# The causal mask of the prompt's attention: an addition by VectorE in PSUM in the place of a matrix product

## What is computed

```python
s = q @ k.T * HEAD_DIM ** -0.5          # 512 x 512 for each head
s = where(k_pos <= q_pos, s, -inf)      # the causal mask
p = exp(s - max(s)); p = p / sum(p)
o += gate[branch] * (p @ v)
```

## Time and profile before

| what | value |
|---|---|
| median of 3 runs | 2102.17 us (2101.37 to 2103.06) |
| the profiled execution's own time | 2100.33 us |
| its span in the profile | 2098.4 us |
| TensorE busy | 1946.2 us (93% of the span) |
| VectorE busy | 1146.9 us (55%) |
| ScalarE busy | 828.4 us (39%) |
| GpSimd busy | 692.4 us (33%) |
| mean granted TensorE clock | 0.966 of full speed |

### The profile page before, as it was taken

How to read it: one execution, slowest core, us unless ns; L and a number is a source line. 1 busy time by engine, 2 the same in 40 slices (tenths; PEclk the granted TensorE clock), 3 DMA queues, 4 the chain that set the end, 5 groups by cost and what they waited for, 6 DMA issues and landing times. The chain is left out here.

```text
span 2098.4 us, 38046 instructions
## 1 busy us (share of the span) xinstructions
PE 1946.2 (93%) x15341; PEld 1819.3 (87%) x15341; DVE 1146.9 (55%) x1931; ACT 828.4 (39%) x1809; POOL 692.4 (33%) x470
## 2 busy tenths in 40 slices
PE   6999798988889999999999996988987999999998
PEld 6999556987679999999999984678965999999998
DVE  3588755553344555555528876555533455555554
ACT  4594355443433232313146823544444341313130
POOL 2335434230033333333323552443200333343331
PEclk8999899999999999999999997999999999999999
DMA  4310520423322222222222132132342322222221
GB/s 152 102 62 21 163 67 16 112 81 113 109 72 84 87 81 81 81 81 81 81 83 82 62 96 84 50 78 62 102 131 64 95 81 81 81 81 81 87 86 55
DMA packets 200635, 175.75 MB, mean 84 GB/s; under 512 B 11356, under 2 KB 198030, under 8 KB 200334
## 3 DMA queue, kind: packets, MB, share of 16 engines
q1 hardware_dynamic: 200354, 173.30, 27.2%
q10 hardware_dynamic: 108, 0.03, 0.0%
HBM read 162.67 MB, written 10.62 MB: 83 GB/s over the span
## 5 line engine op out<-in xcount | busy, mean ns | idle before, releaser
L427 POOL TENSOR_TENSOR WX<-RAW,WX 128x2048 fp32r<-128x2048 f32 (+2 forms) x48 | 222.5, 4635 | 567.8 <-ACT WX L423 567.8
L2393 DVE TENSOR_TENSOR sq<-sq 128x288 f32<-128x288 f32 x128 | 157.0, 1231 | 196.8 <-ACT sq L2362 196.8
L427 POOL TENSOR_TENSOR m_wl<-RAW,m_wh 128x2048 fp32r<-128x2048 f32 x36 | 166.4, 4623 | 285.1 <-ACT m_wh L423 285.1
L439 PE MATMUL bank<-UH,m_wl 128*128 128x288 f32 x640 | 188.8, 295 | 0.0
L438 PE MATMUL bank<-UL,m_wh 128*128 128x288 f32 x640 | 188.8, 295 | 0.0
L437 PE MATMUL bank<-UH,m_wh 128*128 128x288 f32 x640 | 188.7, 295 | 0.0
L439 PE MATMUL bank<-UH,WX 128*128 128x288 f32 x576 | 170.1, 295 | 0.0
L438 PE MATMUL bank<-UL,WX 128*128 128x288 f32 x576 | 169.8, 295 | 0.0
L437 PE MATMUL bank<-UH,WX 128*128 128x288 f32 x576 | 169.7, 295 | 0.0
L423 ACT ACTIVATE WX<-RAW 128x2048 fp32r<-128x2048 f32 (+1 forms) x48 | 92.0, 1917 | 173.5 <-PE bank L439 150.8
L2415 DVE TENSOR_TENSOR XT<-XT,OT 128x288 f32<-128x288 f32 x128 | 156.3, 1221 | 4.4
(11 more groups left out here) (389 smaller groups left out, 5904.0 us busy)
## 6 DMA issues: line engine op xcount, KB each, us to landing
RAW<-in_w_up SPq DMA_DIRECT2D x32, 1024.0 KB, 5.3
RAW<-in_w_down SPq DMA_DIRECT2D x32, 1024.0 KB, 5.0
RAW<-in_w_in SPq DMA_DIRECT2D x20, 1024.0 KB, 5.2
R<-in_cache_nsa_kv SPq DMA_DIRECT2D x128, 64.0 KB
HT<-in_cache_nsa_kv SPq DMA_DIRECT2D x128, 64.0 KB, 2.7
RAW<-in_w_in SPq DMA_DIRECT2D x6, 1056.0 KB, 5.2
R<-in_cache_nsa_kv SPq DMA_DIRECT2D x48, 128.0 KB, 3.0
out<-R SPq DMA_DIRECT2D x10, 512.0 KB, 5.4
```

Of the source, the lines that this page charges most:

```text
L427: eng.tensor_tensor(S.granule(S.wl, i, w)[:, chunks], S.granule(S.raw, i, w)[:, chunks], S.granule(S.wh, i, w)[:, chunks].bitcast(F32), AL ...
L439: ins = pe.matmul(out, wl[:, c, cols], ah[:, c, n], start=False, stop=(c == KC - 1))
L2393: dve.tensor_tensor(relu[n % 4], relu[n % 4], relu[n % 4], ALU.mult).then_inc(sem("relu_squared"), 1)
```

## The change

The two bf16 products of a unit are taken out of `scores`, the second score product now ends its accumulation and increments `scored`, and VectorE adds the mask before it looks for the maximum: one `tensor_tensor` over the diagonal blocks of both heads, 128 partitions x 2 x 128 elements, PSUM in and out, the mask read from SBUF and repeated over the heads. It goes through `step`, so VectorE waits for its own addition before the `tensor_reduce`. In the constants, the bf16 identity and bf16 mask, each 64 columns of the fp32 array, give way to one fp32 mask of 128 columns, so the array keeps its size and the places of the others.

```diff
@@ _constants
-    put("ident16", _halved(np.eye(P)))
-    put("causal16", _halved(np.where(i[None] > i[:, None], NEG, 0.0)))
+    put("causal", np.where(i[None] > i[:, None], NEG, 0.0))
@@ scores(n), TensorE
                         for v in range(NKV):
                             k = slice(v * HD, (v + 1) * HD)
-                            pe.matmul(bank[2 * (n % 2) + v][:, 0:w], QT[k, g, t * P:w], KT[k, b, 0:w], start=True, stop=False)
-                        for v in range(NKV):
-                            ins = pe.matmul(bank[2 * (n % 2) + v][:, t * P:w], ident16, causal16,
-                                            start=False, stop=True)
+                            ins = pe.matmul(bank[2 * (n % 2) + v][:, 0:w], QT[k, g, t * P:w], KT[k, b, 0:w], start=True, stop=True)
                         ins.then_inc(sem("scored"), 1)
@@ VectorE
                             dve.wait_ge(sem("scored"), n + 1)
                             both = psum[:, n % 2 * 1024:n % 2 * 1024 + 1024].rearrange("p (v k) -> p v k", v=NKV)[:, :, 0:w]
+
+                            own = both[:, :, w - P:w]
+                            step(dve, dve.tensor_tensor(own, own, const("causal").unsqueeze(1).to_broadcast([P, NKV, P]), ALU.add),
+                                 "dve_done")
                             dve.tensor_reduce(nmax[:, 2 * n:2 * n + 2], both, AX, ALU.max, negate=True).then_inc(sem("maxed"), 1)
```

More of the change, by code:

```diff
@@ L23 @@
 F32R = mybir.dt.float32r
-BF16 = mybir.dt.bfloat16
 I32 = mybir.dt.int32
@@ L70 @@
 CONST_W = {}
-def _halved(a):
-    return (np.asarray(a, np.float32).view(np.uint32) >> 16).astype(np.uint16).view(np.float32)
 def _constants():
@@ L202, in build @@
         ident, ones, ones64 = const("ident"), const("ones"), const("ones64")
-        ident16, causal16 = const("ident16").bitcast(BF16), const("causal16").bitcast(BF16)
         G_ATTN, G_MLP, G_HG, G_KC, P_B1, P_LBA, P_OM, P_LNOM, P_HB = 0, 8, 16, 17, 18, 22, 26, 30, 34
```

## The result

The changed kernel takes 2115.98 us (median of 4 runs, 2113.22 to 2116.99) against 2102.61 us: 13.4 us slower. The ratio of the runs is 1.0062, its 95% interval 1.0045 to 1.0079. Forecast were 2114 us and 12.0 us.

The account below looks back on a forecast made before the run. Two loops through the engines, not TensorE's busy time, were taken to bound the kernel; addition delays less the earlier `scored` and slack gave 6.0 and 5.9 us in two layers, 12.0 on 2102.17: 2114 us, range 2108 to 2120.

Parts of the forecast that it names:

- loop B: Scores, maximum, exponentials, ScalarE's copy, turning products, later scores: once for two units, 6.75 us at 512 columns, 0.24 more after.
- loop A: VectorE and ScalarE, once a unit: maximum, exponentials, reciprocals, next maximum; 2.80 us at 512 columns, 0.46 more after.
- The faster rival: TensorE's list is the bound, the addition hides in VectorE's idle time: 7.7 us less, 2094.5; chance 0.07.
- The addition, 0.46 us: VectorE's mask addition and wait for itself delay each unit's maximum by 0.46 us, 0.42 of it the addition.
- The upper bound of 0.52: VectorE's addition at its dearest: a two-input form of 479 ns plus 0.04 for the wait.
- the rival with 2108 us: VectorE's wait for itself is free, the addition costs 0.33 instead of 0.46: 5.7 us off the sum; chance 0.05.
- `scored` 0.22 us earlier: Without TensorE's two mask products `scored` comes 0.22 us earlier, helping loop B once in two units, loop A not.
- The walk through the units: Following both loops through the first layer's 32 units: last maximum 6.0 us late; second layer 5.9.
- TensorE's list, 0.12 us for two products: The two mask matmuls fill about 0.12 us of TensorE's list, worth something only where TensorE is the limit.
- Nothing outside the loops: What follows the block covers nothing, constants and DMA unchanged, rest of the kernel as before: 0 us.
- The rival in which the clock falls: TensorE's clock falls in the narrow units, about 0.5 us over loop A each: 8 us on top, 2122; chance 0.08.
- The delay mostly absorbed: `scored` 0.32 earlier, addition about 0.33: loop B pays nothing, 1.8 us a layer, 2106; chance 0.08.

Follow-up runs that it names:

- e5: Changed kernel with ScalarE's copy of head 0 of unit n - 3 ahead of the exponentials of unit n; 2106.2 us, ratio 1.0017 to the kernel before.
- e9: Kernel before, mask products kept, with ScalarE's copy of head 0 ahead of the exponentials; 2086.9 us, ratio 0.9921.
- e4: Changed kernel with VectorE's reciprocals of unit n - 1 behind the copy of unit n; 2107.4 us, ratio 1.0022 to the kernel before.
- e8: Kernel before, mask products kept, with VectorE's reciprocals one unit late; 2095.8 us, ratio 0.9960.
- e6: Changed kernel with both orders changed, copy ahead of the exponentials and reciprocals one unit late; 2082.0 us, ratio 0.9897 to the kernel before.
- e7: Kernel before, mask products kept, with both orders changed, copy ahead of the exponentials and reciprocals one unit late; 2083.9 us, ratio 0.9902.
- e1: Kernel before without its mask products and with no addition, diagonal block left unmasked; 2096.6 us, ratio 0.9977.
- e2: Changed kernel with the mask products put back, so the mask is added twice; 2119.9 us, ratio 1.0086 to the kernel before.
- e3: Changed kernel with the addition executed twice, each with its wait; 2144.1 us, ratio 1.0204 to the kernel before.
- e11: e7 with the mask by products only in a layer's first four units and by addition in the other 28; 2079.9 us, ratio 0.9886 to the kernel before.
- e10: Kernel before with the mask products ahead of the score products, scores accumulated onto the mask; 2104.6 us, ratio 1.0001.

## Why the prediction was right

The time, the direction and the size were right, and so were the steps that carry them. Point by point:

**What bounds the kernel.** Right. The busy time said TensorE, the waits said two loops. e5 and e9 take loop B away, e4 and e8 loop A. TensorE's list sets the pace where both are gone (e6, e7), and in e9, whose loop A is the shorter one without the addition. The faster rival (TensorE as the bound, 2094.5) is refuted by the result, and by e1: without any mask VectorE still waits for the scores 16 times, 8.0 us in the first layer, and the first units keep their 2.80.

**The addition, 0.46 us.** Right: 0.42 us for the instruction (420 ns, mean of 64; 418 in the row that it was taken from) and 0.46 to the maximum. The upper bound of 0.52 was not needed. Loop A grew by 0.47 us (2.80 to 3.27), not by 0.33, and the rival with 2108 us falls with it. That rival took the wait as free and the maximum as starting early. The rule of the Trainium skill on the page "VectorE: DVE Perf Modes", section "The DRAIN you can't avoid", grants the first and denies the second. Both together would cost no less than the instruction's 0.42 us, so the rule is 0.05 us from what was measured, and doesn't lead to 0.33. No run took the wait away alone, so its own price isn't shown.

**`scored` 0.22 us earlier.** Right: the addition starts 1.17 us behind its scores where the maximum started 1.38 behind them. e1 prices it at 6 us, e2 at 4 (4.7 from first to last maximum in the two layers).

**The walk through the units.** 6.0 us a layer were forecast for the last maximum. The lateness along the way is as walked: 1.9 us at the sixth unit, 2.2 at the eighth, 3.2 at the sixteenth and 4.4 at the twenty-fourth (1.9, 2.1, 3.1 and 4.3 were forecast). At the last maximum, measured are 0.25 in the first unit and 5.93 from first to last in the first layer (83.77 against 77.84), and 0.25 and 5.89 in the second (83.76 against 77.87): 6.2 and 6.1. The paces are as forecast: 3.27 in the first units, 3.50 at 512 columns, 2.88 at 384 (308.49 to 314.25 for two), 2.31 at 256 and 1.83 at 128. e3 doubles the addition and adds 13.8 us a layer to the way from first to last, where 10.5 had been expected; 2.9 of the 3.3 in excess stand in three steps at a low clock.

**TensorE's list, 0.12 us for two products.** Mis-sized: 0.07 (3.18 against 3.11 us for a unit in e7 and e6). I had read it from the first start of the mask to the first start of the next group, and had not seen that this next group is 0.05 shorter behind a mask (0.97 against 1.02). It didn't enter the sum, but it made the forecast of e7 against e6 wrong (6 to 7 us expected, 1.9 measured).

**Nothing outside the loops.** Not quite. The sum ended at the last maximum and took the rest of the block as unchanged. That rest, from the last maximum to the next block's first work, went from 5.54 to 6.82 us and from 5.47 to 5.97 in the two layers, 1.8 us in all. Its products are slower because the clock falls there, at 352.3 in the first layer:

```profile
352.30:359.30 7.00, 5.57 (x28) 2.68 (x28) 1.97 (x7) 2.41 (x9) 1.75 (x4) 0.50 0.00 0
```

```profile
354.14 0.66 PE L1347 MATMUL bank<-cst,R 128*128 128x128 f32 x2 [0.59 <-ACT R L1393]
...
355.98 0.70 PE L1361 MATMUL bank<-R 128*64 128x128 f32 x4
```

In the second layer the clock is 1.00 until 1396 and 0.50 from 1398: such products took 0.43 and 0.44 at first and 0.69 at 1397.13, and the tail is shorter (5.97). e2 has the same pace of 1.83 us in the last units, keeps the full clock and takes 5.54 and 5.48. The term was put at nothing, and one of the signs of being wrong that the forecast had named, a granted clock that leaves 1.00 behind the first units, did come. The rival in which the clock falls had the event right and its place wrong: not in the narrow units but from the last one's turn on. Why it falls there isn't shown. In e5, with the addition, it is 0.50 in both tails; in e8, with the products, 0.83 in one and 1.00 in the other; the kernel before also waits for copies in its tail and has 1.00. With this term the two blocks make 12.3 + 1.8 = 14.1 us, of which the medians show 13.4. The sum was 2.1 us short by the blocks (0.3 in the walk, 1.8 in the tail); that the medians show only 1.4 of it is scatter and no merit of the forecast.

**The delay mostly absorbed** (2106): refuted. It needed a cheap addition and 0.32 us from `scored`; both bounds were at the wrong end.

## What to carry to other kernels

The two products of the mask cost TensorE's list 0.07 us a unit here, and in the old order their price was the delay of the semaphore behind them (0.22 us). The addition on VectorE cost 0.46 us on the path, so it pays only where VectorE has slack in the loop that sets the pace. Look for that loop before you move work: an engine at 95% busy here was waiting in a loop of three engines, and two moves in the order of the lists (a copy ahead of the exponentials that don't need it, reciprocals that nobody is waiting for one unit later) were worth 20 us (e7), more than three times what the mask's products cost (6 us, e1). After such a move the sums of all earlier choices are to be made again: the addition that cost 12 to 19 us in the other orders costs nothing that the runs can tell in the new one, and in 28 of 32 units it is the better choice by the trace (e11's block is 1.4 us shorter than e7's).

## What was not expected of the hardware

- Two bf16 matmuls of 128 columns take 0.07 us of TensorE's list behind fp32 products and ahead of fp32 transposes, and 0.22 us ahead of fp32 products of 64 rows (e10). The cause is open.
- TensorE's clock can fall with TensorE busy for well over half of the time. In the changed kernel it stays at 1.00 with 9.65 of 12 us busy (335 to 347) and 5.10 of 7.3 (345.0 to 352.3), then falls at 352.3. In e3, with the units 2.30 us apart instead of 1.83, it falls at 349.4, behind 2.34 of 4 us busy (345 to 349), is back at 1.00 from 356 to 360 (2.51 of 4 us) and falls again. The busy share of a stretch at the low clock can't be set beside one at the full clock, since the same products take longer in it: e3's 16 us with a mean of 0.71 show 12.64 us busy, the same 0.8 as in the changed kernel. The Trainium skill, "TensorE: Matmul & The Clock Gate", section "A second HAM failure mode: psum-queue depth-cycling", names short gaps between groups as a cause of a swinging clock. e3 agrees with it (down, up and down again between 349 and 367 us); the changed kernel shows one fall, at the end of the block.
- An addition on VectorE that writes PSUM takes as long as one that writes SBUF: 420 and 418 ns for 128 x 256.
